# Another order table for the merged stage of a two-layer hybrid decoder step

## The chip, the cores and the metric

One Trainium2 chip, one core. The metric is the device time of one execution in microseconds (us); lower is better. The kernel before took 1944.37 us as the median of three runs, which lay between 1939.79 and 1945.36.

## The reference

Two layers of a hybrid decoder, one step for two groups that share the weights: a prompt of 512 positions and 8 samples of one position each, behind 2048 cached ones. What one layer computes, cut to what matters:

```python
h = rms_norm(x, norm_mix_pre)
proj = h @ w_in                                # q, k, v of three branches, gates; r, k, v, LoRA inputs
o_nsa = g0 * o_cmp + g1 * o_sel + g2 * o_win   # compressed, selected and window attention
s = s * w_t + (s @ a_t) b_t + v_t k_t          # RWKV-7 recurrence over t, y_t = s r_t
mixed = concat(o_nsa, o_rwkv) @ w_out
x = x + rms_norm(mixed, norm_mix_post)
u = rms_norm(x, norm_ffn_pre) @ ffn_w_up       # gate and value halves
f = (gelu(causal_conv(gate)) * val) @ ffn_w_down
x = x + rms_norm(f, norm_ffn_post)
```

For the samples the compressed and the selected rows come from a paged cache through a page table. Everything is float32.

## The kernel before

Each layer runs through an input projection, a **merged stage**, an output projection and the feed-forward part. The dense parts split weights and inputs into a high and a low half and use three matmuls for one product. The change touches only the merged stage, in which everything between the two projections is computed at once.

The merged stage consists of threads, lists of steps in their own fixed order, each step with its engine: the recurrence of the samples (`step_thread`, digit 0 in the table), the chunked scan of the prompt in four threads (`rwkv_threads`: front 1, back 2, side 3, tail 4; four chunks of 128 positions), the early split of the first output weight (`early_thread`, 5), ScalarE's share of the page loads (`page_thread`, 6), the prompt's attention (`att_thread`, 7), the samples' attention (`sample_thread`, 8) and SyncE's loads (`load_thread`, 9). `ORDER` (L429) is a string of 777 digits; `merged_order` (L438) reads it from left to right, takes the next step of the thread that each digit names, and gives the list `PAIRED` (L469). Digit 9 only takes a place: SyncE's program is not laid out by the table.

The three compute engines walk the same list and execute those steps that are theirs: TensorE at L1645 (334 steps in a layer), ScalarE at L2038, VectorE at L2780. Both layers use the same list. Each engine works strictly in the order of its own steps and waits on semaphores of the others, so the table sets who stands behind whom in each queue, and no more.

Steps that the later text names, with TensorE's lines:

- the prompt's attention goes unit by unit (24 of them): scores (L1514), mask (VectorE L2621, L2622), exp (ScalarE L2000), weigh (VectorE L2626 to L2631), turn (the transpose, L1521), evac (ScalarE L2006), values (L1531, L1535);
- the scan, for each chunk: lora_w (L1280), pair products pairb and pairk (L1372), tm (a turn of the operands, L1397), inv (L1406) and dbl (L1417, L1419) for five levels, rhs, solve, advance, yout, and at its end mean (L1474), var (L1479) and, in the last chunk, vspread (L1487) and VectorE's out (L2578 to L2583). VectorE's scaled (L2520 to L2524) prepares the first products of a chunk;
- the samples: chunks (compression, L1550), sel_k (L1592) and sel_v (L1637), eight sets each of selected keys and values, sel_out (L1642).

TensorE divides its array by the operands of a matmul: 128 by 128, 64 by 64 (the two heads of a tile beside each other), 64 by 128, 128 by 64 or 128 by 32. Matmuls on float32 operands stand in the trace as two records each.

The cached rows come through three slots in rotation: set u may be loaded when TensorE has used set u - 3. Of the sixteen page loads of a selected set SyncE issues twelve and ScalarE four (L952 to L972, called for ScalarE at the table's digit 6):

```python
        if u >= USLOT:
            eng.wait_ge(S["u_used"], u - USLOT + 1)
```

When the list is done, VectorE signals `mixed` (L2793), and TensorE, which waits for it, begins the output projection (L1125 to L1127). The first output weight needs its split: whi on ScalarE (L1753), wlo on VectorE (L2293), both steps of thread 5.

Of the kernel before, what the change touches and what calls it, by code (L numbers as in the profile page):

```python
# [423 lines left out]
def warm_thread(att):  # L424
# [1 line left out]
    return [(("warm", i, "ones"), "PE", 0.9, [att[-2][0]]) for i in range(WARM)]  # L426


ORDER = ("700077897880870901788801788071088787087789907088788008887717180088710817071800889177108091071807170898108279788878283338"  # L429
         "283227782288327288782727827977788278277883389227838282383887121789782178227977728288327718727882827817878891177188882812"  # L430
         "218728978227217872183722892128872271728872787887287828274787882422487243878882842747988888973732227892732888233787827334"
         "273828837282871238777228712887372778178178927162217821789172217788278811729872728722812277781278281272282822776827872847"
         "493242846782824272326982273727367237924232738722742378231971727392371112277682121772728121971712211977262722782618728732"
         "822928227288272782782882778262987224872868447822822722882996976824773272672772747823297633272878272327972376872277829234"
         "772272274272222723727332273722764477874548447475873874888")


def merged_order():  # L438
# [3 lines left out]
    at, order = [0] * len(rows), []  # L442
    for c in ORDER:
        i = int(c, 16)
# [2702 lines left out]
```

## Time and profile before

| what | us |
|---|---|
| median of three runs | 1944.37 |
| the profiled execution | 1941.26 |
| its span, first to last instruction | 1939.4 |
| TensorE busy | 1868.8 |
| VectorE busy | 1349.0 |
| ScalarE busy | 864.3 |

The profile counts an engine as busy from the start of an instruction to its modelled end. Matmuls are pipelined, so a row's duration is longer than the distance to the next start; the distance between the starts of two steps is what a step costs. The merged stage of the first layer begins at 170.2 us and ends when the first output matmul starts at 538.35; that of the second begins at 1128.7.

### The profile page before, as it was taken

The numbers are of one execution on the slowest core, as the hardware profiler recorded it, in microseconds if no ns is written. First come the engines' busy times: TensorE is split into PE (matmuls) and PEld (weight loads), VectorE is DVE, ScalarE is ACT, GpSimd is POOL, SyncE is SP. The second block draws the span as 40 slices with busy tenths as digits, with TensorE's granted clock in tenths as the row PEclk, the third lists the DMA queues.
The fourth block names the chain that finished last, engine by engine and source line by source line (L and its number), as shares of the span: only waits on it lengthen the run. The fifth ranks groups of instructions, "written<-read, shape, count | busy, mean of one in ns | idle before, by whom it ended". The sixth has DMA issues, their size and how long they took to land.

```text
span 1939.4 us, 53758 instructions
## 1 busy us (share of the span) xinstructions
PE 1868.8 (96%) x22168; PEld 1734.6 (89%) x22168; DVE 1349.0 (70%) x2250; ACT 864.3 (45%) x1692; POOL 72.1 (4%) x143
## 2 busy tenths in 40 slices
PE   7999999998999999999999999999989999999997
PEld 7999888776889999999999988887767999999997
DVE  3475867887637999952356767688876389999423
ACT  3223345554435566652232234545536365656421
POOL 0000000000000111200000000000000001111000
PEclk9999999999999999999999999999999999999999
DMA  6325544144332233233332255432442222332332
GB/s 223 91 86 169 154 119 155 47 127 115 102 105 81 95 108 101 78 101 96 104 143 91 77 186 165 126 110 73 125 130 87 92 99 88 109 99 88 94 95 90
DMA packets 153014, 214.30 MB, mean 110 GB/s; under 512 B 18497, under 2 KB 118338, under 8 KB 151362
## 3 DMA queue, kind: packets, MB, share of 16 engines
q1 hardware_dynamic: 134050, 200.38, 32.9%
q10 hardware_dynamic: 18720, 10.49, 1.8%
q8 instruction: 175, 2.87, 0.6%
q14 instruction: 69, 0.57, 0.1%
HBM read 202.58 MB, written 16.59 MB: 113 GB/s over the span
## 4 chain that ended last, share of the span: by engine, by line
PE 69%; DVE 17%; ACT 6%; issue 4%; DMA 2%; ACTq 1%; SPq 0%; DVEq 0%
PE ps L1125 11%; PE ps L1127 11%; PE ps L1126 11%; PE ps L1696 5%; PE ps L1698 5%; PE ps L1697 5%; PE ps L1550 3%; DMA ring<-in_w 2%; PE ps L1417 1%; PE ps L1406 1%; PE ps L1158 1%; PE ps L1159 1%; PE ps L1521 1%; DVE arena L2622 1%; ACTq L972 1%
## 5 line engine op out<-in xcount | busy, mean ns | idle before, releaser
L2293 DVE TENSOR_TENSOR ring_lo<-ring,ring_hi 128x1024 fp32r<-128x1024 f32 x82 | 100.4, 1224 | 187.4 <-ACT ring_hi L1753 185.1
L1127 PE MATMUL ps<-hf_hi,ring_lo 128*128 128x260 f32 x704 | 198.9, 283 | 0.0
L1127 PE MATMUL ps<-in_hi,ring_lo 128*128 128x260 f32 x672 | 189.7, 282 | 0.0
L1753 ACT ACTIVATE ring_hi<-ring 128x1024 fp32r<-128x1024 f32 x82 | 86.7, 1059 | 206.8 <-DMA ring<-in_w 203.6
L1127 PE MATMUL ps<-hm_hi,ring_lo 128*128 128x260 f32 x480 | 137.1, 286 | 0.0
L1127 PEld LDWEIGHTS ps<-hf_hi,ring_lo 128*128 128x128 f32 x704 | 132.6, 188 | 0.0
L1125 PE MATMUL ps<-hf_hi,ring_hi 128*128 128x260 f32 x448 | 127.5, 285 | 0.4
L1127 PEld LDWEIGHTS ps<-in_hi,ring_lo 128*128 128x128 f32 x672 | 126.6, 188 | 0.0
L1126 PE MATMUL ps<-hf_lo,ring_hi 128*128 128x260 f32 x448 | 126.6, 282 | 0.0
L1125 PE MATMUL ps<-in_hi,ring_hi 128*128 128x260 f32 x416 | 119.8, 288 | 1.7 <-DVE ring_lo L2293 1.7
L2293 DVE TENSOR_TENSOR ring_lo<-ring,extra_hi 128x1024 fp32r<-128x1024 f32 x42 | 51.4, 1225 | 97.4 <-ACT extra_hi L1753 95.9
L1126 PE MATMUL ps<-in_lo,ring_hi 128*128 128x260 f32 x416 | 117.7, 283 | 0.0
L2000 ACT ACTIVATE arena<-ps,arena 128x128 f32<-128x128 f32 (+3 forms) x128 | 66.1, 526 | 97.6 <-DVEq L494 92.2
L2237 POOL COPY arena<-arena 128x2 f32<-128x2 f32 x44 | 36.8, 837 | 1721.3 <-DVEq L494 1422.2
L1753 ACT ACTIVATE extra_hi<-ring 128x1024 fp32r<-128x1024 f32 x42 | 44.5, 1059 | 116.2 <-DMA ring<-in_w 115.6
L1127 PEld LDWEIGHTS ps<-hm_hi,ring_lo 128*128 128x128 f32 x480 | 91.9, 192 | 0.0
L1125 PEld LDWEIGHTS ps<-hf_hi,ring_hi 128*128 128x128 f32 x448 | 84.3, 188 | 2.5 <-issue 2.5
L1126 PEld LDWEIGHTS ps<-hf_lo,ring_hi 128*128 128x128 f32 x448 | 84.3, 188 | 0.0
L1696 PE MATMUL ps<-t_hi,e_r 128*128 128x260 f32 x288 | 81.3, 282 | 1.1 <-ACT ps L2114 1.1
L1697 PE MATMUL ps<-t_lo,e_r 128*128 128x260 f32 x288 | 81.3, 282 | 0.0
L1125 PEld LDWEIGHTS ps<-in_hi,ring_hi 128*128 128x128 f32 x416 | 78.3, 188 | 2.8 <-issue 2.5
L1126 PEld LDWEIGHTS ps<-in_lo,ring_hi 128*128 128x128 f32 x416 | 78.3, 188 | 0.3
(560 smaller groups left out, 6095.1 us busy)
## 6 DMA issues: line engine op xcount, KB each, us to landing
ring<-in_w SPq DMA_DIRECT2D x158, 512.0 KB, 3.6
arena<-in_w SPq DMA_DIRECT2D x44, 512.0 KB, 3.5
extra<-in_kv_cmp SPq DMA_DIRECT2D x96, 128.0 KB, 2.3
arena<-in_kv_cmp SPq DMA_DIRECT2D x80, 128.0 KB, 2.7
slot<-in_kv_cmp SPq DMA_DIRECT2D x80, 128.0 KB, 2.5
out_win_old<-in_win SPq DMA_DIRECT2D x16, 511.0 KB, 4.2
slot<-in_k_sel SPq DMA_DIRECT2D x72, 64.0 KB, 2.1
extra<-in_k_sel SPq DMA_DIRECT2D x72, 64.0 KB, 1.9
```

The lines of the kernel that those rows point to most:

```text
L972: eng.dma_start(dst[:, i, :], src[l * N_POOL + r]).then_inc(done, 16)
L1125: mmul(out, wh, hi[:, k, cols], start=(at == 0), stop=False)
L1126: mmul(out, wh, lo[:, k, cols], start=False, stop=False)
L1127: last = mmul(out, wl, hi[:, k, cols], start=False, stop=(ci == len(chunks) - 1 and at == k1 - 1))
L1550: last = mmul(out, w1ss[l][c][:, k, :], slot[:, :, c, k, :], start=(k == 0), stop=(k == STRIDE // 2 - 1))
L1696: mmul(out, wh[:, w], hi[:, k, :], start=new, stop=False, skip_group_check=True)
L1697: mmul(out, wh[:, w], lo[:, k, :], start=False, stop=False, skip_group_check=True)
L1698: last = mmul(out, wl[:, w], hi[:, k, :], start=False, stop=(k == HK - 1), skip_group_check=True)
L1753: A(w_high(l, n), w_place(l, n), ACT.Copy).then_inc(S["w_hi"], 1)
L2000: o.go(A(pp[:, g, cols], ps[:, 4 + g, cols], ACT.Exp, bias=nm[:, q:q + 1], accum_out=sums[:, q:q + 1]))
L2237: o.go(g.tensor_copy(cout[:, i, :], gx[:, i % 2, SEQ:SEQ + 2]))
L2293: v.tensor_tensor(w_low(l, n), w_place(l, n), w_high(l, n), SUB).then_inc(S["w_lo"], 1)
```

## The change

Only the string is replaced. It has again 777 digits, and each digit as often as before, so every engine executes the same steps with the same waits; their order in the three queues differs over the whole stage. SyncE's order is untouched.

```diff
-ORDER = ("700077897880870901788801788071088787087789907088788008887717180088710817071800889177108091071807170898108279788878283338"
...
-         "772272274272222723727332273722764477874548447475873874888")
+ORDER = ("978090780988870770878800789870070887788087771078880787107997871781887171810017078007878701780081017018888771800818787237"
...
+         "747227322722923722728263224774744863774749887745747887588")
```

The end of the stage, read through the threads, for each engine in its order:

```
TensorE before:  ... solve1, turn22, rknorm, advance1, scores23, yout1, values22, mean, sel_v5,
                 var, sel_v6, turn23, vspread, sel_v7, values23, sel_out1
TensorE after:   ... solve1, sel_v4, advance1, yout1, turn22, mean, scores23, var, sel_v5,
                 values22, sel_v6, sel_v7, turn23, vspread, values23, sel_out1
VectorE before:  mask23, weigh23, vrec, wlo, out, sel_add1, smp_done
VectorE after:   mask23, vrec, weigh23, out, wlo, sel_add1, smp_done
ScalarE before:  pages35, ycopy, exp23, msub, whi, vroot, evac23, sel_vo1, heads
ScalarE after:   ycopy, evac22, msub, pages35, exp23, vroot, whi, evac23, sel_vo1, heads
```

Values set 7 is load 35. Before, sel_v4 stands 24 steps of TensorE ahead of sel_v7, after, 10.

## Rows read from the trace of the kernel before

**Rows 1.** The page's busy times: us (share of the span) x instructions.
```profile
PE 1868.8 (96%) x22168; PEld 1734.6 (89%) x22168; DVE 1349.0 (70%) x2250; ACT 864.3 (45%) x1692; POOL 72.1 (4%) x143
```
**Rows 2.** Windows: length; busy PE, PEld, DVE, ACT, POOL (x instructions); clock; DMA.
```profile
170.00:538.30 368.30, 348.98 (x6075) 292.11 (x6075) 283.82 (x559) 180.19 (x424) 0.00 (x0) 1.00 0.41 123
...
190.50:230.00 39.50, 34.97 (x490) 31.20 (x489) 33.44 (x54) 14.22 (x40) 0.00 (x0) 1.00 0.52 160
```
**Rows 3.** TensorE's time line: start, us from first start to last end.
```profile
198.97 2.94 PE L1550 MATMUL ps<-slot,smp 128*128 128x128 f32 x24
...
203.63 1.16 PE L1280 MATMUL ps<-arena 64*128 64x128 f32 x8
204.71 1.16 PE L1550 MATMUL ps<-extra,smp 128*128 128x128 f32 x8
205.80 1.11 PE L1336 MATMUL ps<-arena 64*64 64x32 f32 x31
...
230.67 1.10 PE L1397 MATMUL ps<-cst,arena 64*64 64x64 f32 x32
231.60 0.50 PE L1372 MATMUL ps<-arena 64*64 64x128 f32 x6
...
246.03 1.15 PE L1406 MATMUL ps<-nsa,arena 64*64 64x64 f32 x32
247.10 1.17 PE L1550 MATMUL ps<-arena,smp 128*128 128x128 f32 x8
```
**Rows 4.** TensorE's waits, first layer; last row second: us in total, times, longest.
```profile
PE ps L1521 <- DVEq L494: 2.8, 5, 1.3
...
PE ps L1372 <- DVEq L494: 2.0, 4, 1.4
PE ps L1592 <- DMA extra<-in_k_sel: 1.4, 1, 1.4
...
PE ps L1592 <- DMA slot<-in_k_sel: 1.2, 1, 1.2
...
PE ps L1592 <- DMA extra<-in_k_sel: 2.7, 1, 2.7
```
**Rows 5.** SyncE's time line: twelve page loads of key sets 1 and 7.
```profile
386.99 8.20 SPq L972 DMA_DIRECT2D extra<-in_k_sel  x12
...
436.49 6.09 SPq L972 DMA_DIRECT2D extra<-in_k_sel  x12
```
**Rows 6.** ScalarE's page loads of key set 7, and TensorE's read of it.
```profile
447.57 1.82 ACTq L972 DMA_DIRECT2D extra<-in_k_sel  x4
...
451.67 1.07 PE L1592 MATMUL ps<-extra,arena 128*32 128x512 f32 x8 [1.40 <-DMA extra<-in_k_sel]
```
**Rows 7.** Time line of the front: a mask, a weighting, the first pair product.
```profile
214.63 0.69 DVE L2622 TENSOR_REDUCE arena<-ps 128x4 f32<-128x512 f32 x1
...
218.75 0.69 DVE L2631 TENSOR_TENSOR arena<-arena 128x512 f32<-128x512 f32 x1
...
229.74 1.09 PE L1372 MATMUL ps<-arena 64*64 64x128 f32 x16 [1.39 <-DVEq L494]
```
**Rows 8.** Time line at the stage's end, VectorE and TensorE.
```profile
530.49 1.22 DVE L2293 TENSOR_TENSOR ring_lo<-ring,fourth_hi 128x1024 fp32r<-128x1024 f32 x1
...
531.76 1.09 PE L1487 MATMUL ps<-cst,extra 128*64 128x128 f32 x16
...
536.69 0.70 DVE L2300 TENSOR_TENSOR hm_lo<-hm,hm_hi 128x520 fp32r<-128x520 f32 x1 [0.76 <-ACT hm_hi L1757]
...
538.35 0.39 PE L1125 MATMUL ps<-hm_hi,fourth_hi 128*128 128x260 f32 x1 [2.46 <-DVEq L2793]
```
**Rows 9.** TensorE's read of values 0; SyncE's page loads of values 3 and 6.
```profile
475.51 1.09 PE L1637 MATMUL ps<-arena,smp 128*32 128x128 f32 x32
...
477.57 7.29 SPq L972 DMA_DIRECT2D arena<-in_v_sel  x12
...
502.68 8.31 SPq L972 DMA_DIRECT2D arena<-in_v_sel  x12
```

More of the change, by code:

```diff
@@ L426, in warm_thread @@
     return [(("warm", i, "ones"), "PE", 0.9, [att[-2][0]]) for i in range(WARM)]
-ORDER = ("700077897880870901788801788071088787087789907088788008887717180088710817071800889177108091071807170898108279788878283338"
[L430 to L434, printed above, removed]
-         "772272274272222723727332273722764477874548447475873874888")
+ORDER = ("978090780988870770878800789870070887788087771078880787107997871781887171810017078007878701780081017018888771800818787237"
+         "837222397893723282387288277282987278382873728818878277879282781383271872877892228783981877718788772788882787722891181218"
+         "727811182282827872828987278227271827238271872872877822728299448738787788242228282288772878428872824782288723398277283228"
+         "787847783732828743898227783287238277831182727872832189716878287892811287281378122818771828178221721788272791228622877848"
+         "742498724972326796247779232332226283272382327724734272183977227831776229377621271277281722117899671227728197282877812212"
+         "122812281722287822227878272244748222729284827862227867782827687826278327472727976933322783728737632297227787232732428272"
+         "747227322722923722728263224774744863774749887745747887588")
 def merged_order():
```

## The prediction

> **What bounds the kernel now.** I read the busy shares first, then the table of windows over the two merged stages (one in each layer), then TensorE's waits in them, and at the end single stretches of the time line. TensorE is busy 96% of the span, VectorE 70% [rows 1]; the reader is to see that no other engine is near it. The order table sets nothing outside the merged stages. The first takes 368.3 us, at full clock, with TensorE busy 349 us and VectorE 284 us [rows 2]; the second is the same table again. So the stage is TensorE's own sequence of 334 steps plus about 20 us in which it waits. "Busy" here hides the price of changing the form in which the array is divided, because a step is only a little longer and a gap a little wider. Three things can therefore move: that price, the waits, and the end of the stage, where TensorE waits 2.46 us for VectorE's last step before the output projection begins [rows 8].
>
> **The changes of form: counted and priced.** Both tables hold the same 777 entries, so every instruction stays; only the neighbours change. I walked both tables through the threads and gave every TensorE step its form, rows by columns (128 by 128 for compression chunks, transposes, norms; 64 by 64 for the scan; 64 by 128 for scores and LoRA; 128 by 64 for values; 128 by 32 for the sample group's reads). Of 333 neighbouring pairs in one layer, 237 change form before and 218 after: 19 fewer. The price comes from equal steps in different company. Five chunk steps in a row (24 matmuls in the row shown, 16 more behind it) run from 198.97 to 203.63, 4.66 us; one alone between other forms runs from 204.71 to 205.80, 1.09 us [rows 3]. With c for the step itself, 5c + e = 4.66 and c + e = 1.09 give c = 0.89 and e = 0.20 us for entering and leaving. A 64 by 64 step of 32 matmuls takes 0.93 us from start to start among its own kind (230.67 to 231.60) and 1.07 between chunks (246.03 to 247.10), so e = 0.14 [rows 3]. One change is one leaving and one entering, 0.14 to 0.20 us. The removed ones lie mostly beside 64 by 64 steps, so I take 0.15: 19 x 0.15 = 2.9 us less per layer. The ends are 0 (if the engine hides them in waits that grow by as much) and 19 x 0.20 = 3.8.
>
> The rows show a price on both sides of a change [rows 3]. The Trainium skill (TensorEngine Tiling (Array Packing), section Tiling Modes, Key Properties) says that changing the tiling mode drains the engine, and gives no duration. If a drain cost the whole 0.39 us that a single matmul is shown to last at 538.35 [rows 8], the 19 changes would be 7.4 us per layer and 15 us in all. The rows of equal steps say 0.14 to 0.20 [rows 3], and the sum goes by them.
>
> **The rows of selected keys.** TensorE waits 1.4 + 1.2 us in the first layer and 2.7 in the second for key sets 6 and 7 [rows 4]. In the first layer SyncE issued its twelve of the sixteen loads of key set 7 from 436.49 to 442.6, but ScalarE's four went out only from 447.57 to 449.4, and TensorE started at 451.67, 2.3 us behind them [rows 5, 6]. The new table puts ScalarE's loads of set 6 right behind those of set 5, some 16 us earlier, and those of set 7 before the transpose of unit 16 is copied out. What is late next is SyncE: its sets follow each other every 8.25 us (386.99 to 436.49, six sets) [rows 5]. From the end of the window read that frees the slot of key set 1 to key set 7 the new table has 59 us of TensorE's steps. SyncE needs 1.0 us after a release to begin (476.60 to 477.57 [rows 9]), six sets at 8.25, 6.1 for the last and 2.3 to land, also 59 us; the 3 to 5 us of other waits in that stretch give it room. I take 2.7 us saved per layer; the ends are 0 (SyncE sets the same wait) and 2.7. A shorter wait for values set 2 stays: in the new table ScalarE issues three sets nearly in a row just ahead of it, as before.
>
> **The front.** From 190.5 to 230 VectorE works with hardly a pause (33.4 of 39.5 us, small gaps between dependent operations among the rest), and TensorE waits for it, 1.39 us ahead of the first pair product [rows 2, 7]. The new table puts one more attention unit's mask and weighting ahead of the scan's first scaling: two operations of 0.7 us in the mask and one behind three of 0.2 in the weighting, about 2.6 us more on VectorE [rows 7]. Against that, TensorE has 1.6 us more steps of its own ahead of the first product, and the samples' recurrence, which opens VectorE's long run, can start 0.5 us earlier because one chunk step more covers the first transpose. That leaves 0.5 us, of which I take 0.3 per layer as not made up later; the ends are -1 and +2.6.
>
> **The end of the stage.** Here the change costs. (a) The split of the first output weight, 1.22 us on VectorE, stood ahead of the scan's output step, in the time in which VectorE waited for TensorE; now it stands behind it, between the first low half of the input (536.69) and the last two small steps [rows 8]. From the end of the variance spread (531.76 + 1.09) to the first output matmul (538.35) it took 5.5 us without it; with it, 6.7. (b) The read of values set 7 was 1.0 us of TensorE work behind the variance spread; it is now ahead of it, so it no longer covers any of these 6.7 us: 1.0. (c) Values set 7 uses the slot that values set 4 frees. In the old table 24 us of steps lie between the two, now 8.9. SyncE starts 1.0 us after a release, issues for 6.1 to 8.3 us, mostly 7.3, and the last rows take 2.3 to be used [rows 5, 6, 9]: 9.4 to 11.6 us against 8.9. The wait is 0.5 to 2.7. Part of it would have been there anyway, since the last unit's transpose waits for its weighting (ScalarE now issues four loads, 1.8 us, between the scan's mean subtraction and the exponential): I take 1.0. The sum is 1.2 + 1.0 + 1.0 = 3.2 us per layer, from 2.2 to 5.
>
> **The sum.** Per layer -2.9 - 2.7 + 0.3 + 3.2 = -2.1 us; both layers use the table, so -4.2. The other waits (short pieces, of which the rows for transposes and pair products are the largest [rows 4]) I leave as they are, because the steps between each producer and its consumer are about as many in both tables. The profiled execution took 1941.26 us, 1939.4 of it span, so it becomes 1937.1. The runs shown had a median of 1944.37, 3.1 above the profiled one; from the median it is 1940.2. I forecast 1940, a gain of 0.2%. A measurement of this kernel can tell about 0.3% (5.8 us) from no change.
>
> **Rivals.**
> 1. The waits in the middle shrink too. In the first layer the transposes of the attention wait 2.8 us and the pair products 2.0 for VectorE's queue [rows 4]. The new table often keeps scores and their transpose further apart (nine steps instead of six for unit 2). If two thirds of 4.8 us go in each layer, that is -6.4, and the total is -10.6: 1934. For it: the attention unit is further ahead at the front and the form changes fell as well. Against it: VectorE's load is the same and its waits may only move.
> 2. Slower: SyncE's loads become the bound. It decides if a set takes over 8.25 us from start to start; one at the end of the stage was issued for 8.31 alone [rows 9]. Then the waits at keys 6 and 7 stay (0 in place of -2.7) and that at values 7 is 2.7 in place of 1.0: -2.9 + 0 + 0.3 + 4.9 = +2.3 per layer, +4.6: 1949. For it: SyncE's six sets from 387 on ran back to back [rows 5]. Against it: the other waits give it room in the middle.
> 3. The fewer changes give nothing: the short gaps they leave are taken up by VectorE's answers, which come no earlier. Then -2.7 + 0.3 + 3.2 = +0.8 per layer, 1946. For it: most links of the scan have only a step or two between product and answer. Against it: the long rows of chunk steps wait for nobody.
>
> **How the numbers follow.** The forecast case gets 0.42, rival 1 0.32, rival 2 0.14, rival 3 0.12. The forecast case alone spans 1935 to 1944. Faster by over 0.3% (below 1938.5): nearly all of rival 1 and a fifth of the forecast case, 0.40. Slower by over 0.3% (above 1950.2): a good third of rival 2, a little of rival 3, and mishaps in an order of 777 entries that no row foretells, 0.10. The rest, 0.50, is within it. The range 1930 to 1949 takes in rival 1 down to its larger gains and rival 2's point.
>
> **What would show it.** In the profile after: a stage of 366 to 367 us; a chunk or scan step as long as now, but fewer of the long ones; no wait above 1 us for key sets 6 and 7; the split of the output weight between the scan's output and the last copies, and 4.5 to 5.5 us of waiting ahead of the first output matmul in place of 2.46; a wait of about 1 us for values set 7. The prediction is wrong if the stage is under 364 us (rival 1), or if TensorE waits longer for the sets than now (rival 2), or if times outside the two stages move.

## The result: slower by 0.55%, and most of it is TensorE's clock

The changed kernel takes 1952.72 us (median of 7 runs, 1948.81 to 1955.6), the kernel before 1942.01 (7 runs, 1939.79 to 1945.36) beside it: a ratio of 1.0055, 95% interval 1.0045 to 1.0064. The forecast was 1940, the range ended at 1949, and slower had a chance of 0.1. The profiled execution of the changed kernel has a span of 1953.8 us against 1939.4, 14.4 us more; it is the slowest of its seven, so its trace shows somewhat more loss than the 10.7 us of the medians.

The page looks unchanged. TensorE is busy 5.4 us longer for the same number of instructions, and the row of the granted clock, in tenths of full speed, is 9 in all 40 slices, as it was before:

```profile
PE 1874.2 (96%) x22168; PEld 1745.6 (89%) x22168; DVE 1348.9 (69%) x2250; ACT 864.5 (44%) x1692; POOL 72.2 (4%) x143
...
PEclk9999999999999999999999999999999999999999
```

A slice of that row is 49 us, so a few microseconds at half clock stay in the same digit. The mean clock of the run does show it: 0.988 against 0.996, and 0.988 to 0.991 in all seven runs of the changed kernel, where the runs of the kernel before beside the experiments have 0.993 to 0.997. The table of windows, laid over the first merged stage and then over short stretches, finds the place. Its columns are length, busy time of the five engines, clock, DMA share and GB/s, as in [rows 2], whose first row answers to the first here:

```profile
169.90:544.60 374.70, 351.38 (x6076) 296.98 (x6076) 283.67 (x559) 180.39 (x424) 0.00 (x0) 0.98 0.41 122
...
229.30:236.10 6.80, 6.11 (x82) 6.11 (x84) 4.78 (x12) 2.89 (x4) 0.00 (x0) 0.50 0.86 255
389.70:393.10 3.40, 3.40 (x67) 3.28 (x62) 3.00 (x6) 2.02 (x3) 0.00 (x0) 0.50 0.37 92
468.20:471.60 3.40, 3.40 (x18) 1.56 (x16) 2.79 (x10) 1.56 (x5) 0.00 (x0) 0.50 0.20 58
543.30:550.10 6.80, 5.50 (x25) 5.51 (x26) 6.27 (x13) 4.16 (x7) 0.00 (x0) 0.50 0.22 83
...
1195.20:1202.00 6.80, 5.76 (x76) 5.76 (x78) 4.82 (x12) 2.89 (x4) 0.00 (x0) 0.50 0.77 244
1355.70:1359.10 3.40, 3.40 (x61) 3.28 (x56) 3.04 (x5) 1.79 (x3) 0.00 (x0) 0.50 0.42 121
1434.20:1437.60 3.40, 3.23 (x30) 3.23 (x32) 2.73 (x6) 1.41 (x4) 0.00 (x0) 0.50 0.18 53
1509.30:1516.10 6.80, 4.69 (x21) 4.69 (x22) 6.27 (x12) 4.98 (x8) 0.00 (x0) 0.50 0.34 133
```

Each layer has four stretches at 0.50, the lower of the two levels (1.2 GHz): 6.8, 3.4, 3.4 and 6.8 us, together 20.4 us, at the same steps in both layers. The kernel before has one of 3.4 us in each layer, just behind the stage's end, and none inside its stages (every run also has some 9 to 11 us at 0.50 at its very end). Its longest wait, 2.73 us for the rows of key set 7 in the second layer, was not followed by a fall, as the window from that wait on shows:

```profile
539.10:542.50 3.40, 3.40 (x17) 3.40 (x17) 3.40 (x5) 3.25 (x5) 0.00 (x0) 0.50 0.35 125
...
1408.40:1415.00 6.60, 3.87 (x141) 2.92 (x141) 3.34 (x6) 4.39 (x10) 0.00 (x0) 1.00 0.49 141
```
```profile
1411.16 1.07 PE L1592 MATMUL ps<-extra,arena 128*32 128x512 f32 x8 [2.73 <-DMA extra<-in_k_sel]
```

What TensorE did before a fall stands in its time line (start, us from first start to last end). At the front of the stage:

```profile
226.84 0.61 PE L1535 MATMUL ps<-arena 128*64 128x128 f32 x8
229.99 1.97 PE L1397 MATMUL ps<-cst,arena 64*64 64x64 f32 x32 [2.54 <-DVEq L494]
231.75 3.62 PE L1372 MATMUL ps<-arena 64*64 64x128 f32 x32
...
238.33 1.10 PE L1397 MATMUL ps<-cst,arena 64*64 64x64 f32 x32
```

The scan's first transposes (L1397) wait 2.54 us for VectorE in one piece. Then 32 matmuls take 1.97 us where the same step takes 1.10 at 238.33, as it did before the change [rows 3]. Before the change the idle time at the front came in smaller pieces, 1.39 us at this place [rows 7] and 1.28 us ten microseconds ahead of it:

```profile
219.56 0.66 PE L1521 MATMUL ps<-cst,arena 128*128 128x128 f32 x4 [1.28 <-DVEq L494]
```

Over the whole stage the idle time did not only change its pieces, it grew: 374.70 - 351.38 = 23.3 us without work on TensorE, where it was 368.30 - 348.98 = 19.3 [rows 2].

TensorE's waits of the first stage (us in total, times, longest), which answer to [rows 4]:

```profile
PE ps L1125 <- DVEq L2793: 4.4, 1, 4.4
PE ps L1417 <- DVEq L494: 3.3, 6, 1.2
PE ps L1372 <- DVEq L494: 2.6, 3, 1.6
PE ps L1397 <- DVEq L494: 2.5, 1, 2.5
...
PE ps L1521 <- DVEq L494: 1.0, 2, 0.6
```

The three rows for key sets (L1592, DMA) are gone, in both layers. ScalarE's loads for sets 6 and 7 now go out long before they are read, and the read of set 7 at 448.6 us waits for no load. In the time line of ScalarE's and SyncE's queues, which answers to [rows 5, 6]:

```profile
434.51 1.98 ACTq L972 DMA_DIRECT2D slot<-in_k_sel  x4
441.43 1.90 ACTq L972 DMA_DIRECT2D extra<-in_k_sel  x4
```
```profile
436.47 7.34 SPq L972 DMA_DIRECT2D extra<-in_k_sel  x12
```

The end of the stage, which answers to [rows 8]: values set 7 waits 1.21 us, the split of the output weight (L2293) stands behind the first low half (L2300), and the first output matmul waits 4.40 us where it waited 2.46:

```profile
534.84 1.08 PE L1637 MATMUL ps<-slot,smp 128*32 128x128 f32 x32 [1.21 <-DMA slot<-in_v_sel]
...
536.88 1.09 PE L1487 MATMUL ps<-cst,extra 128*64 128x128 f32 x16
...
541.80 0.70 DVE L2300 TENSOR_TENSOR hm_lo<-hm,hm_hi 128x520 fp32r<-128x520 f32 x1 [0.76 <-ACT hm_hi L1757]
542.42 1.22 DVE L2293 TENSOR_TENSOR ring_lo<-ring,fourth_hi 128x1024 fp32r<-128x1024 f32 x1
...
544.60 0.59 PE L1125 MATMUL ps<-hm_hi,fourth_hi 128*128 128x260 f32 x1 [4.40 <-DVEq L2793]
```

To compare kernels I set the start of some steps against the first matmul of their stage (L1499), from the starts of TensorE's matmuls in each time line. All are microseconds; two numbers are the two layers. The last column is the sum of everything outside the two stages, up to TensorE's last matmul.

| kernel | tm0 of scan 0 | inv 2 of scan 0 | inv 1 of scan 2 | scores 18 | rhs 0 of scan 3 | first output matmul | outside |
|---|---|---|---|---|---|---|---|
| before | 60.5, 60.4 | 85.0, 85.2 | 241.7, 242.3 | 291.7, 292.5 | 340.2, 340.8 | 368.2, 369.0 | 1190.6 |
| changed | 60.0, 60.3 | 88.0, 88.2 | 245.6, 245.8 | 292.5, 293.8 | 342.5, 344.8 | 374.6, 375.5 | 1192.0 |
| e1_fill_front | 60.1, 60.3 | 85.8, 86.2 | 242.8, 243.1 | 289.7, 290.5 | 339.7, 340.4 | 373.9, 372.1 | 1191.9 |
| e2_fill_both | 60.1, 60.3 | 85.9, 86.2 | 243.5, 243.9 | 290.4, 290.8 | 340.5, 340.7 | 371.5, 372.1 | 1186.6 |
| e3_before_fill_end | 60.5, 60.4 | 85.0, 85.2 | 241.7, 242.8 | 291.2, 292.3 | 339.5, 340.5 | 367.5, 368.7 | 1187.6 |
| e5_new_old | 60.0, 60.4 | 86.8, 87.4 | 244.5, 245.4 | 295.1, 297.4 | 343.5, 345.7 | 371.5, 373.9 | 1191.0 |
| e6_old_new | 60.4, 60.3 | 84.8, 85.1 | 241.6, 242.2 | 288.7, 289.5 | 338.4, 339.6 | 370.1, 370.2 | 1190.7 |
| e7_mid | 60.5, 60.4 | 85.0, 85.2 | 241.7, 242.3 | 289.0, 289.3 | 339.0, 342.5 | 367.0, 370.5 | 1192.4 |
| e11_mid_fill_both | 60.5, 60.4 | 85.0, 85.2 | 241.7, 242.3 | 288.8, 289.5 | 338.5, 339.7 | 366.5, 367.7 | 1188.1 |
| e12_new_all_covered | 60.1, 60.4 | 85.9, 86.2 | 243.6, 244.4 | 290.5, 291.3 | 340.5, 341.5 | 368.5, 369.5 | 1187.8 |

### The profile page after: what moved, and what is told of

Its sections match the earlier page's. It is cut to its first block, busy times and chain, and to the rows that moved or that the text cites. A ratio compares the mean times of both kernels' runs of the same rounds, so it can differ in the third digit from the quotient of the medians.

```text
span 1953.8 us, 53758 instructions
## 1 busy us (share of the span) xinstructions
PE 1874.2 (96%) x22168; PEld 1745.6 (89%) x22168; DVE 1348.9 (69%) x2250; ACT 864.5 (44%) x1692; POOL 72.2 (4%) x143
## 4 chain that ended last, share of the span: by engine, by line
PE 67%; DVE 20%; ACT 5%; issue 4%; DMA 2%; SPq 1%; ACTq 0%; DVEq 0%
PE ps L1125 11%; PE ps L1127 11%; PE ps L1126 11%; PE ps L1696 5%; PE ps L1698 5%; PE ps L1697 5%; PE ps L1550 3%; DMA ring<-in_w 2%; PE ps L1417 1%; PE ps L1158 1%; DVE arena L2631 1%; PE ps L1159 1%; PE ps L1419 1%; DVE arena L2622 1%; PE ps L1521 1%
## 5 line engine op out<-in xcount | busy, mean ns | idle before, releaser
L2293 DVE TENSOR_TENSOR ring_lo<-ring,ring_hi 128x1024 fp32r<-128x1024 f32 x82 | 100.4, 1225 | 185.6 <-ACT ring_hi L1753 182.7
L2293 DVE TENSOR_TENSOR ring_lo<-ring,extra_hi 128x1024 fp32r<-128x1024 f32 x42 | 51.4, 1225 | 97.7 <-ACT extra_hi L1753 96.3
L1417 PEld LDWEIGHTS ps<-nsa 64*64 64x64 f32 x1280 | 67.4, 133 | 18.7 <-issue 11.0
```

Of the source, the lines that this page charges most:

```text
L1417: last = mmul(ps[r, 0, cj * CH:(cj + 1) * CH], qq[r, c, j, :], zz[r, c, j, :], start=True, stop=True)
L2293: v.tensor_tensor(w_low(l, n), w_place(l, n), w_high(l, n), SUB).then_inc(S["w_lo"], 1)
```

## The experiments

The theory after the result: the new order gathers more of TensorE's idle time into single pieces, the clock falls behind them, and the half-clock time costs more than the order saves. The rivals: the longer waits alone; the stage's end alone; a change of form that is worth less than priced. In the first three runs TensorE is kept at work in a wait and the order stays. The extra matmuls write a free bank of PSUM, or one that the next step overwrites, and are read by nobody.

**e1_fill_front.** The changed order, with one edit ahead of the first transpose of a layer's first scan:

```diff
                         src = (bt, kt, y)[n]
+                        if sc == 0 and n == 0:
+                            for _ in range(11):
+                                mmul(ps[:, 2, 0:P], ones[:], ones[:], start=True, stop=True)
```

> The changed kernel with 11 extra 128-row matmuls of ones into a free bank just before the transpose tm0 of chunk 0 of each layer, where TensorE otherwise waits 2.5 to 2.9 us in one piece; the output is not touched by them. Clock theory (idle time in one piece lowers the granted clock, and that costs more than the idle time): the 6.8 us at half clock behind this place vanish, the clock stays at 1.00 in 229 to 237 us, each stage is about 3 us shorter, and the time falls by 4 to 7 us against the changed kernel, to 1946 to 1949 us. Rival (the time is lost to the waits alone): the waits are as long with or without the fillers, so the time stays within 1 us of 1952.7 or rises by the fillers' own 2.4 us per layer where they outlast the wait.

Measured: 1946.82 us (11 runs), ratio to before 1.0021 [1.0012, 1.0030]; the changed kernel stands at 1.0055. So 6.6 us of the loss go by the ratios (0.0034 x 1942). The time line and the window of the same place:

```profile
228.61 2.72 PE L1389 MATMUL ps<-ones 128*128 128x128 f32 x22
231.26 1.15 PE L1400 MATMUL ps<-cst,arena 64*64 64x64 f32 x32
232.25 1.92 PE L1372 MATMUL ps<-arena 64*64 64x128 f32 x32
```
```profile
230.00:240.00 10.00, 9.52 (x208) 8.94 (x207) 8.46 (x21) 3.90 (x6) 0.00 (x0) 1.00 0.61 190
```

The transposes start as late as without the fillers (60.1 us into the stage against 60.0), so no waiting was taken away. Yet the transposes take 1.15 us and not 1.97, the pair products 1.92 and not 3.62, and inv 2 comes 2.1 us earlier. The fall of 3.4 us at 390 us went as well, in both layers. In the first layer that at 467 us stayed and one of 3.4 us came at 534.8, ahead of the stage's end; the second layer has only that of the end.

**e2_fill_both.** The same, and 19 such matmuls ahead of the wait for the stage's last result:

```diff
+                for _ in range(19):
+                    mmul(ps[:, 4, 0:P], ones[:], ones[:], start=True, stop=True)
                 pe.wait_ge(S["mixed"], l + 1)
```

> The changed kernel with the 11 matmuls of the run before and 19 more of the same kind ahead of the wait for the scan's last result at the end of the stage, where TensorE waits 4.4 us. Clock theory: both 6.8 us periods at half clock vanish, two of 3.4 us in mid stage stay; the first output matmuls after the stage run at full clock, which gives 3 us more per layer; 1940 to 1945 us in all. Rival (waits alone): 1951 to 1956 us, no gain.

Measured: 1943.78 us (11 runs), ratio 1.0003 [0.9994, 1.0012]: with the changed order and its waits as they were, the time is that of the kernel before. Three falls of 3.4 us are left inside its stages, one in the first layer and two in the second. The output matmuls behind the stage start 0.12 us apart in this kernel; in the changed kernel without the fillers 0.21 to 0.22 us (the second fence):

```profile
537.83 2.40 PE L1661 MATMUL ps<-ones 128*128 128x128 f32 x20
540.29 0.39 PE L1125 MATMUL ps<-hm_hi,fourth_hi 128*128 128x260 f32 x1
540.51 0.28 PE L1126 MATMUL ps<-hm_lo,fourth_hi 128*128 128x260 f32 x1
540.63 0.28 PE L1127 MATMUL ps<-hm_hi,ring_lo 128*128 128x260 f32 x1
```
```profile
544.98 0.42 PE L1126 MATMUL ps<-hm_lo,fourth_hi 128*128 128x260 f32 x1
545.20 0.42 PE L1127 MATMUL ps<-hm_hi,ring_lo 128*128 128x260 f32 x1
```

The time outside the stages falls from 1192.0 to 1186.6 us, 5.4 us. Of the two stretches of 6.8 us, 5.5 and 4.7 us lie behind the first output matmul (544.60 to 550.1, and 1511.4 to 1516.1), so each microsecond at half clock costs about 0.53 us there.

**e3_before_fill_end.** The kernel before, with 11 of these matmuls at its end of the stage.

> The kernel before, its order untouched, with 11 matmuls of the same kind ahead of the same wait at the end of the stage, which is 2.46 us there. Clock theory: the only half-clock period of its layers (3.4 us at 539 and at 1498 us) vanishes, each is worth about 1.7 us, so 1938 to 1940 us beside 1942 for the kernel before. Rival (the clock's fall costs nothing where it stands): 1942 us or, with the fillers outlasting the wait, up to 1 us more.

Measured: 1940.72 us (11 runs), ratio 0.9986 [0.9977, 0.9995]; the time lies above the 1938 to 1940 that I had expected, because the 1943.33 beside it was higher than the 1942 that I had set; the gain of 2.7 us is within the expected 2 to 4. Outside the stages 3.0 us went for two stretches of 3.4, 0.44 for each microsecond. The kernel before was paying this price too, unseen. So the fair comparison for e2 is this kernel: with the long waits of both orders covered, the changed order is still 0.17% (3.3 us) behind. Of the loss of 0.55% about 0.38 is then the clock, some two thirds.

**e4_old_front.** The old order until inv 2 of the first scan, then the changed one; against the changed table:

```diff
-ORDER = ("978090780988870770878800789870070887788087771078880787107997871781887171810017078007878701780081017018888771800818787237"
-         "837222397893723282387288277282987278382873728818878277879282781383271872877892228783981877718788772788882787722891181218"
+ORDER = ("700077897880870901788801788071088787087789907088788008887717180088710817071800889177108091071807170898108279788878283338"
+         "283227782288327288782727827977788278277883389227838277717777781383271872877892228783981877718788772788882787722891181218"
```

> The order of the kernel before until the second inverse step of chunk 0 (rwkv 0, inv 2), and from there the order of the changed kernel, with 227 changes of form instead of 218. Clock theory: the wait of 2.5 us before tm0 is broken up again, its half-clock period goes, those at 390, 468 and 543 us stay: some 3 us less per stage, 1945 to 1948 us. Rival 1 (the 19 removed changes of form save what was forecast, and the front costs nothing): 9 changes come back, 1.4 us per layer more, 1955 us. Rival 2 (the end of the stage alone makes the loss): 1952 to 1955 us.

Measured: 1972.84 us (5 runs), ratio 1.0151 [1.0137, 1.0165]: slower than either parent, which no theory expected. At the seam the old order has not yet done eight steps that the new one has (attention unit 4 from its mask to its values, the scores of unit 5, and an activation of the next scan), and they now run in one row. VectorE and ScalarE answer each other there while TensorE has nothing:

```profile
263.14 1.97 PE L1521 MATMUL ps<-cst,arena 128*128 128x128 f32 x8 [5.08 <-DVEq L494]
```
```profile
260.00:270.20 10.20, 5.90 (x34) 4.68 (x36) 3.52 (x6) 5.45 (x16) 0.00 (x0) 0.50 0.00 0
```

One wait of 5.08 us, and 10.2 us at half clock around and behind it. Inv 1 of scan 2 comes at 255.2 us, some 10 us later than in the changed kernel. The run says nothing of the front's own worth, but it says what a hybrid must look like. The next are cut where both orders have done the same steps but one or two.

**e5_new_old** and **e6_old_new.** The orders cut at inv 1 of scan 2, where they differ by one load: each half of the change alone.

> The changed order until the step inv 1 of scan chunk 2 (246 us after the stage's first matmul), then the order of the kernel before: 220 changes of tile form, so 17 of the 19 that the change saves. The two orders have done the same steps at this point but for two loads. Clock theory: the changed first half is level with the old one in steps and loses what its half-clock periods cost, the old second half then runs as it did (126.5 us and one drop of 3.4 us at its end); stage 371.5 to 372.5 us, in all 1944 to 1948 us, slower than before and 5 to 8 us better than the changed kernel. Rival (form changes save 0.15 us each and only the tail loses): 1937 us, faster than before.

> The opposite halves: the old order until inv 1 of scan chunk 2, then the changed one; 235 changes of tile form. Clock theory: the first half without a half-clock period (241.7 us), the second as in the changed kernel (129 us with the drops at 468 and 543 us), so a stage of 370 to 371 us and 1948 to 1951 us in all. Rival (the loss is the front's alone): 1942 us or less.

Measured: 1947.92 us (7 runs), 1.0030 [1.0019, 1.0041], and 1944.03 us (11 runs), 1.0015 [1.0006, 1.0024]. Both halves lose, the first more, although it has 17 of the 19 removed changes (14 of 15 by the count below). The intervals of the two overlap, so that order of the losses is only likely. The stages are as expected, but for the second of e5 (371.5 and 373.9 us, where I had expected up to 372.5; 370.1 and 370.2). The total of e6 is 4 us under its expectation: I had added the end's longer fall, and outside the stages its profiled execution is level with the kernel before (1190.7 us against 1190.6).

**e7_mid.** The changed order only from inv 1 of scan 2 to the mask of unit 18. Two lines of the table differ from the kernel before:

```diff
-         "493242846782824272326982273727367237924232738722742378231971727392371112277682121772728121971712211977262722782618728732"
+         "493242846782824272326982273727367237929382327724734272183977227831776229377621271277281722117899671227728197282877812212"
-         "822928227288272782782882778262987224872868447822822722882996976824773272672772747823297633272878272327972376872277829234"
+         "122812281722287822227878273826287224872868447822822722882996976824773272672772747823297633272878272327972376872277829234"
```

> The kernel before with the changed order only in the stretch from inv 1 of scan chunk 2 to the mask of attention step 18, where the waits for the key sets 6 and 7 stood: 236 changes of tile form, one fewer than before. Theory (this is the part of the change that works as forecast, 2.7 us per layer from the key sets): the stretch takes 47 us and not 50, the time is 1936 to 1938 us. Rival (a wait gathered at 468 us drops the clock and takes it back, or the time comes out again as a longer wait behind it): 1941 to 1943 us.

Measured: 1939.88 us (12 runs), 0.9989 [0.9980, 0.9998]. The stretch takes 47.3 and 47.0 us, and 50.0 and 50.2 before: 2.7 and 3.2 us saved, as forecast. Behind it the profile has a wait of 1.61 us and 3.4 us at half clock, so both theories hold in part and the time lies between their ranges. Its profiled execution is one of the two slowest of its twelve: at the end of both stages it has 6.8 us at half clock, behind the same wait of 2.46 us that is followed by 3.4 us in the kernel before. In the first layer key set 7 still waits 1.61 us here, now for SyncE's twelve loads, which are issued until 442.2 and read at 445.27, while ScalarE's four went out by 437.9. So only 1.0 of that layer's 2.7 us come from the key sets, and the rest from other waits.

**e8_mid_fill_end.** The same with the 11 matmuls of e3 at the end.

> The kernel of the run before with the 11 extra matmuls of ones ahead of the wait for the last result of the scan. If both theories hold (2.7 us per layer from the key sets, 1.3 us per layer from the clock at the end): 1934 to 1936 us, faster than both kernels. If either fails, 1938 to 1941 us.

Measured: 1937.57 us (12 runs), 0.9981 [0.9972, 0.9990]. It lies between the two expectations, faster than both kernels.

**e9_extra_same_form** and **e10_extra_other_form.** The price of a change of form by itself, in the kernel before. The extra product is overwritten by the one behind it; e9 has it in the form of its neighbours, e10 in another:

```diff
+                        if part == 0:
+                            mmul(W4[:, c, 0, CH * half:CH * (half + 1)], ones[:], ones[:, 0:CH], start=True, stop=True)
                         for k in range(4 * part, 4 * part + 4):
```
```diff
+                            mmul(W4[0:HD, c, 0, CH * half:CH * (half + 1)], ones[0:HD, 0:HD], ones[0:HD, 0:CH], start=True, stop=True)
```

> The kernel before, with one extra matmul of ones ahead of 32 of the 64 compression products of a layer (those with part 0), written where the product behind it overwrites it, in the same 128 by 128 form: no change of tile form is added. All theories: 64 extra matmuls of 64 columns at about 0.06 us (half of the 0.11 us that those of 128 columns take in the trace), less what falls into waits: 1 to 4 us more than before, 1943 to 1946 us.

> The same with the extra matmul in the 64 by 64 form, so that each of the 64 adds two changes of tile form, 128 in all. The price of the forecast (0.15 us a change, all on the path): 19 us above the run before, 1962 to 1965 us. Rival 1 (a change costs 0.10 us, what the trace shows as the longer gap on each side of a 64 by 64 step): 13 us above it. Rival 2 (a change costs next to nothing, since work behind it catches up in the waits): less than 5 us above it.

Measured: 1949.91 us (4 runs), 1.0044 [1.0028, 1.0060], and 1954.16 us (4 runs), 1.0066 [1.0050, 1.0082]. The extra product itself runs as two matmuls and takes 0.17 us (178.97 to 179.14), not the 0.06 that I had expected, so e9 is 4 to 7 us over its expectation; what counts is the difference of the two. One place in both time lines, first e9, then e10:

```profile
178.08 1.06 PE L1552 MATMUL ps<-extra,smp 128*128 128x128 f32 x8
178.97 0.33 PE L1550 MATMUL ps<-ones 128*128 128x64 f32 x2
179.14 2.03 PE L1552 MATMUL ps<-arena,smp 128*128 128x128 f32 x16
181.10 0.71 PE L1514 MATMUL ps<-nsa 64*128 64x128 f32 x8
```
```profile
178.33 1.06 PE L1552 MATMUL ps<-extra,smp 128*128 128x128 f32 x8
179.32 0.33 PE L1550 MATMUL ps<-ones 64*64 64x64 f32 x2
179.57 2.08 PE L1552 MATMUL ps<-arena,smp 128*128 128x128 f32 x16
181.59 0.71 PE L1514 MATMUL ps<-nsa 64*128 64x128 f32 x8
```

From the chunk ahead to the step behind it is 3.02 us in e9 and 3.26 in e10: 0.24 for two changes, 0.12 each. At its place a change of form is real and near the price of the forecast.

That place is not all of them, though. Of the 64 extra products 38 stand behind a step of the 128 by 128 form. From eight matmul records ahead of the product to eight behind it, e10 takes 0.23 us more than e9 there (the median), for two changes. But 14 stand behind a 64 by 64 step, where the extra product adds no change and e10 is 0.11 us faster, and 12 behind 64 by 128 or 128 by 64, where it adds one and costs 0.03. So e10 adds 2 x 38 + 12 = 88 changes and not 128, and the sum over the 64 places is 3.1 us in the first layer and 4.4 in the second, which has a fall of 3.4 us at 1139.0 that e9 has not. Of these, 3.2 and 2.5 us arrive in the two stages: in the first layer, where neither run has a fall, the whole of it. In the medians it is 4.3 us, with four runs each and intervals that just overlap. The extra products stand among the compression steps, whose long rows wait for nobody, so this says what a change costs, and not what taking one away saves elsewhere.

**e11_mid_fill_both.** The order of e7, the end's matmuls, and eight more ahead of the first pair product of scan 3:

```diff
+                            if sc == 3 and c == 0:
+                                pe.wait_ge(T["s_ok"], 2 * sc)
+                                for _ in range(8):
+                                    mmul(ps[:, 0, 0:P], ones[:], ones[:], start=True, stop=True)
```

> The kernel before with the changed order in the stretch from inv 1 of scan chunk 2 to the mask of attention step 18, the 11 extra matmuls of ones at the end of the stage, and 8 more ahead of the first pair product of scan chunk 3, where TensorE waits 1.6 us and the clock then falls for 3.4 us at 463 us. Clock theory: that period goes too, 1.7 us per layer, 1933 to 1936 us, and faster than the kernel with the end's matmuls alone (1937.6). Rival (that period has another cause than this wait): 1937 to 1940 us with the half-clock period still there.

Measured: 1935.57 us (6 runs), 0.9963 [0.9950, 0.9975], the fastest of all. Both stages run at full clock. The pair products, first in e7 and then here:

```profile
462.90 3.33 PE L1372 MATMUL ps<-arena 64*64 64x128 f32 x32 [1.61 <-DVEq L494]
```
```profile
461.05 2.03 PE L1367 MATMUL ps<-ones 128*128 128x128 f32 x16
463.01 1.96 PE L1376 MATMUL ps<-arena 64*64 64x128 f32 x32
```
```profile
169.00:538.00 369.00, 354.66 (x6132) 298.42 (x6131) 286.01 (x564) 182.17 (x426) 0.00 (x0) 1.00 0.42 124
1120.00:1500.00 380.00, 363.81 (x6209) 307.45 (x6208) 292.35 (x572) 184.47 (x429) 0.00 (x0) 1.00 0.42 124
```

The products are 1.4 us faster, but in the first layer rhs 0 of scan 3 follows scores 18 after 49.7 us, and after 50.0 in e7: what is won there is mostly lost to VectorE's answers behind it. In the second it is 50.2 us against 53.2, where e7 also has a wait of 2.08 us for values and a second fall. Against e8 the intervals overlap; how much the eight matmuls bring is not settled.

**e12_new_all_covered.** The changed order until the mask of unit 18, the old one behind it, and all three fillings:

> The changed order until the mask of attention step 18 and the old one behind it, 219 changes of tile form, with extra matmuls of ones in three waits: 11 before tm0 of scan chunk 0, 8 before the first pair product of scan chunk 3, 11 at the end. It differs from the fastest kernel so far (0.9963 of the kernel before) in its first half alone: 17 fewer changes of form per layer, and the wait gathered before tm0, now covered. If a change of form is worth the forecast's 0.15 us on the path: 4 to 5 us less than that kernel, 0.994 of the kernel before. If it is worth the 0.03 to 0.05 us that the extra matmuls showed: 1 us less from the forms, given back by a half-clock period at 390 us where that remains (1 to 3 us), so 0.996 to 0.998.

Measured: 1937.39 us (7 runs), 0.9970 [0.9959, 0.9981], no better than e11 and perhaps a little worse. With its waits at the front covered, the first half with 17 fewer changes (13 by the count below) reaches inv 1 of scan 2 at 243.6 and 244.4 us, e11 at 241.7 and 242.3. One fall of 3.4 us per layer is left in it, at 387 us in the first.

## Why the forecast was wrong, step by step

**The step that failed** is the sum itself: it takes both stages "at full clock" [rows 2] and has no term for the clock. A mean of 1.00 over 368 us was true of the old order and was silently carried over to the new one; the other waits were left "as they are", by their sum, while their lengths changed. What replaced it: the changed kernel has 20.4 us at half clock in each layer, and the kernel before 3.4.

What the falls inside a stage cost is read from e1, which has none up to inv 1 of scan 2: 242.8 and 243.1 us, where the changed kernel with 10.2 us at half clock takes 245.6 and 245.8, 2.8 and 2.7 more. The third fall, ahead of rhs 0 of scan 3, costs nothing that can be seen in the first layer: from inv 1 to rhs 0 it is 96.9 us, and 96.8 and 97.4 in e11, which has no fall. In the second layer it is 99.0, so at most 1.7 to 1.9 us. Outside the stages the two kernels differ by 1192.0 against 1190.6. That is 6.9 to 8.8 us of clock in the 14.4 us of the two profiled spans; the rest is steps and waits, and differences between executions. The medians give a firmer share: the fillings take back 0.52% in the changed order (e2) and 0.14% in the old one (e3), so about 0.38 of the 0.55% is the clock, with an interval of 0.1% to either side on each ratio.

The Trainium skill (TensorE: Matmul & The Clock Gate, section HAM oscillation) tells of a kernel whose tensor engine falls to the lower clock again and again behind waits for data, and counts half of the time at the lower clock as lost. The traces agree with the mechanism, with VectorE's results in the place of DMAs. At the stage's end, where TensorE is the bound, they agree with the price too: 0.53 and 0.44 us per microsecond (e2, e3). Inside the stage it is lower, 2.7 to 2.8 us for 10.2 us up to inv 1 of scan 2, 0.27; that other engines answer no sooner there is the likely reason, and no run separates it.

**Changes of form: -2.9 us per layer forecast, nothing found.** The price at its place was nearly right (0.12 between 128 by 128 steps, I took 0.15). The number was too high: counted on the matmuls of the trace, with each size rounded up to 32, 64 or 128, a stage has 242 changes before and 227 after, 15 fewer and not 19; the prediction gave each step one form, and some steps hold more than one. What failed most is that all of it would reach the end. From inv 2 of scan 0 to inv 1 of scan 2, TensorE has 8 changes fewer (103 against 111), and 34 matmul records fewer, of steps that the front has already done. It is busy 4.0 us less, and the stretch lasts as long; how much of the 4.0 us the changes are is not separated. The first row is the kernel before, the second e1, both at full clock:

```profile
255.20:411.90 156.70, 154.38 (x2548) 128.85 (x2549) 124.26 (x248) 77.68 (x186) 0.00 (x0) 1.00 0.35 107
```
```profile
257.00:414.00 157.00, 150.36 (x2515) 126.57 (x2511) 119.48 (x240) 73.05 (x172) 0.00 (x0) 1.00 0.36 109
```

The time saved on TensorE stands there as waits (6.6 us without work where it was 2.3). With the 0.8 to 1.0 us that the front costs, the first half takes 0.8 to 1.1 us more than the old one (e1, 242.8 and 243.1 against 241.7 and 242.3). This was rival 3, to which I gave 0.12. The Trainium skill's drain at a change of mode (TensorEngine Tiling (Array Packing), section Tiling Modes) is stated without a duration; a change costs 0.12 us here, far from the 0.39 that I had weighed.

**Key sets 6 and 7: -2.7 forecast, -3.1 and -2.2 found** in their stretch (46.9 and 48.0 us in the changed kernel, from inv 1 of scan 2 to scores 18; -2.7 and -3.2 in e7), and in the changed kernel the waits are gone. In the first layer of e6, e7 and e11 one of 1.4 to 1.6 us for key set 7 is back, for SyncE's loads: the room that the forecast left for them was small, 59 us against 59, and the 3 to 5 us of other waits that it added are partly gone. But 1.2 to 1.9 us of it come back up to rhs 0 of scan 3, without any fall of the clock (e11: 49.7 and 50.2 us for what took 48.5 and 48.3). From inv 1 to rhs 0 the net is -1.7 and -1.1 (e11). The forecast ended each term at its own place, and asked only for SyncE's loads what is late next.

**The front: +0.3 forecast.** VectorE's scaling came a little later, and the first product that needs it starts at 60.0 and 60.3 us into the stage (tm0), where it was 59.6 and 59.4 (the first pair product, ahead of tm0 then). So most of the 2.6 us of mask and weighting were made up, and the 0.5 us that the forecast had left over are there as 0.4 and 0.9. But the wait in front of it became one piece. Up to inv 2 the front costs 0.8 to 1.0 us at full clock and 3.0 with the fall.

**The end of the stage: +3.2 forecast, +3.1 found.** From rhs 0 of scan 3 to the first output matmul it was 28.0 and 28.2 us, and is 31.7 and 30.6 with the changed order (e6), 31.0 and 31.4 (e2). The split, the uncovered spread and the wait for values set 7 (1.21 us in the first layer) are all there, and the wait of 4.40 us is just under the 4.5 to 5.5 that I had named. In the changed kernel itself the stretch takes 32.1 and 30.7 us.

**The rivals.** Rival 1 did not come: the transposes' waits fell from 2.8 to 1.0 us, but those at the doublings (L1417) grew from 0.5 to 3.3 us and one of 2.5 stands at tm0. Rival 2 did not come in the changed kernel, whose key sets wait for no load; e6, e7 and e11 show it in one layer, with about half of the 2.7 us that stood there before. That slower could come through the clock stood in no rival.

## What to carry to other kernels

When an order is judged by TensorE's waits, their sum is not enough: lay short windows over each longer one to read the granted clock. The page's row of 40 slices showed none of the eight falls. The length alone doesn't foretell a fall either, so the clock has to be read. Where a wait can't be broken up, a few matmuls of no use in a bank that is free keep the clock up, and cost nothing as long as they end before the wait does; here that alone was worth 0.1% for the kernel before and 0.5% for the changed order, and with the one stretch of the change that worked the kernel became 0.37% faster than before. And a saving that is real at its place (0.12 us for a change of form) isn't yet a saving at the end: here the steps with fewer changes took less time on TensorE, and the stretch that holds them lasted as long, because TensorE then waited for VectorE.

## What the runs showed of the hardware

- The lower clock came in stretches of 3.4, 6.8 and 10.2 us, and some of them began before the wait was over (at 543.3, where it ended at 544.60). Behind a wait of 5.08 us there were 10.2 and behind 4.40 us 6.8. Behind 2.54 and 2.86 us at tm0 there were 6.8 in the changed kernel, and 3.4 behind 2.58 and 2.90 in e5. Behind 2.46 us at the stage's end there were 3.4 in the kernel before and 6.8 in e7.
- It is not the wait's length alone. In the changed kernel a fall at 389.7 follows the wait of 0.93 us shown below, while 2.73 us at 1411.16 in the kernel before had none. The wait of 1.62 us at the pair products of scan 3 had a fall of 3.4 us in both layers of the changed kernel, and none in the second layer of e1 and the first of e2. The fall at 389.7 vanished in both layers when the wait 160 us ahead of it was filled (e1), but stood again in e2, which has the same code up to there. The executions of one kernel differ as well: the eleven of e3 have mean clocks from 0.995 to 0.998. What decides these short falls stays open.

```profile
388.04 1.06 PE L1642 MATMUL ps<-cst,smp 128*128 128x8 f32 x8 [0.93 <-ACTq L494]
```
- A change of form between 128 by 128 steps cost 0.12 us (e9, e10). An extra product in the 64 by 64 form behind a 64 by 64 step was 0.11 us cheaper than one in the 128 by 128 form at the same place, though both orders of forms have one change there.
